# V rows of the paged cache loaded in single bundles among the K loads, and the mixer's steps in another order, in a one-core hybrid decoder step

## The reference, cut to what matters

```python
z = rmsnorm(x) @ w_in                  # 1024 x 3584: rq, rk, rv, rg (4 heads of 128), mq, mk, mv (8 heads of 64)
ret  = retention(rotary(rq), rotary(rk), rv)     # prompt: two chunks of 128; sample: 4 steps on state_ret
moba = block-sparse softmax attention(mq, mk, mv)
       # prompt: 256 own keys; sample: 2048 past keys from cache_k/cache_v by page_table:
       # the 3 best of 8 blocks of 256 (by q . mean k) and the own 4 keys
h = x + concat(norm(ret) * silu(rg), moba) @ w_out
y = h + moe(rmsnorm(h))                # top 4 of 32 experts, 1024 -> 2048 -> 1024
```

## Time and profile before

| | |
|---|---|
| median of 3 runs | 1317.4 us (1314.9 to 1321.56) |
| profiled execution, its own time | 1313.23 us |
| its span | 1311.3 us |
| busy: PE, DVE, ACT, POOL | 1222.4, 387.0, 232.3, 117.6 us |
| DMA moved | 500.64 MB, mean 382 GB/s |
| mixer and router, until the first expert's matmuls | 382.7 us |

### The profile page before, as it was taken

The page is one execution under the profiler, slowest core; times in us unless marked ns, Lnnn a source line. Parts: engine busy times, 40 slices in busy tenths (PEclk is TensorE's granted clock), DMA queues, the critical chain, the costliest instruction groups (busy, mean ns, idle before and its releaser), DMA issues.

```text
span 1311.3 us, 17401 instructions
## 1 busy us (share of the span) xinstructions
PE 1222.4 (93%) x7250; PEld 515.3 (39%) x7250; DVE 387.0 (30%) x551; ACT 232.3 (18%) x528; POOL 117.6 (9%) x117
## 2 busy tenths in 40 slices
PE   7999887658999999999999999999999999999996
PEld 3455443323553443434434343343434343343431
DVE  5999962205232211111211112211111112111113
ACT  3021141201421111101112011111201011211102
POOL 2222335263100000000000000000000000000000
PEclk8999998778999999999999999999999999999999
DMA  9999857873889999999999999999999999999994
GB/s 344 387 345 369 319 168 243 304 257 136 328 329 414 430 428 427 429 428 429 428 428 429 428 428 429 428 429 427 429 429 428 430 427 430 428 428 429 426 428 191
DMA packets 56316, 500.64 MB, mean 382 GB/s; under 512 B 6329, under 2 KB 6609, under 8 KB 27601
## 3 DMA queue, kind: packets, MB, share of 16 engines
q1 hardware_dynamic: 41840, 430.55, 78.4%
q0 software_dynamic: 14432, 69.47, 14.5%
...
## 4 chain that ended last, share of the span: by engine, by line
PE 59%; DMA 25%; DVE 9%; issue 5%; ACT 2%; POOL 1%; another core or an unknown queue 0%; SPq 0%; DVEq 0%; POOLq 0%; ACTq 0%
PE psum L904 22%; DMA arena<-w_gate_up 21%; PE psum L935 12%; DVE arena L1379 6%; PE psum L854 4%; PE psum L836 3%; DMA arena<-w_down 3%; PE psum L574 2%; PE psum L488 2%; PE psum L866 2%; PE psum L682 2%; PE psum L414 1%; PE psum L873 1%; PE psum L842 1%; POOL arena L1845 1%
## 5 line engine op out<-in xcount | busy, mean ns | idle before, releaser
L904 PE MATMUL psum<-arena 128*64 128x512 f32 x1920 | 422.7, 594 | 15.1 <-DMA arena<-w_gate_up 15.1
L904 PEld LDWEIGHTS psum<-arena 128*64 128x64 f32 x1920 | 134.9, 137 | 299.3 <-issue 264.6
L1699 DVE TENSOR_SCALAR arena<-psum 128x512 f32<-128x512 f32 x32 | 22.1, 692 | 682.2 <-PE psum L904 642.9
L935 PE MATMUL psum<-arena 128*64 128x512 f32 x960 | 212.6, 595 | 0.0
L1052 ACT ACTIVATE arena<-psum 64x512 f32<-64x512 f32 (+3 forms) x185 | 94.0, 510 | 406.1 <-PE psum L935 170.7
L1379 DVE STREAM_TRANSPOSE arena<-arena 128x2048 f32<-128x2048 f32 x32 | 121.6, 3946 | 2.7 <-PE psum L474 2.4
L935 PEld LDWEIGHTS psum<-arena 128*64 128x64 f32 x960 | 66.4, 137 | 124.1 <-issue 122.3
L488 PE MATMUL psum<-arena 128*128 128x512 f32 x224 | 107.2, 617 | 0.5 <-issue 0.4
L1270 ACT ACTIVATE arena<-arena 128x512 f32<-128x512 f32 x30 | 18.9, 631 | 418.8 <-DVE arena L1699 418.8
L1052 ACT ACTIVATE arena<-psum,arena 128x128 f32<-128x128 f32 (+2 forms) x182 | 53.8, 398 | 179.2 <-PE psum L488 124.6
L836 PE MATMUL psum<-arena 128*128 128x128 f32 x512 | 77.2, 294 | 0.0
...
## 6 DMA issues: line engine op xcount, KB each, us to landing
arena<-w_gate_up SPq DMA_DIRECT2D x128, 2048.0 KB, 29.7
...
arena<-cache_v,arena POOLq DMA_INDIRECT x64
```

The costliest lines, as they stand in the source:

```text
L904: last = mm(psum[64 * g:64 * (g + 1), b, :], xt[:, 2 * kk + m, lhs], gate_slot[slot][:, m, c:c + 512], start=False, stop=kk == 3 and m == ...
L935: last = mm(psum[64 * g:64 * (g + 1), 2, :], at_sb[:, m, SLOTS * q:SLOTS * (q + 1)], down_slot[slot][:, m, 512 * g:512 * (g + 1)], start=q ...
```

## The change

- V is loaded in single bundles, with a semaphore for each of twelve homes: eight in the K and V storage and four at word 12288, where the prompt scores go later. POOL's order is written out: K units 0 to 18, six V bundles, K units 19 to 24, then four V bundles and two K units in turn, then the rest of V. From unit 16 on K uses three homes instead of four, and two of its former places hold V.
- K units are spread over all 14 prompt parts (`K_PARTS`), and one V set is used at the end of each of the last six parts (`V_PARTS`).
- The sample's matmuls of blocks 1 to 6 stand between the k steps of the second prompt part, in bank 7, with semaphores of their own.
- `choose(0)` and both rotations stand between K transposes on DVE.
- The prompt scores and softmax come after block 6, their transposes and products after the retention products; value sets 8 to 15 stand among them. The transposed probabilities are written over the scores, and `state_ret` is loaded only after the prompt's products (`prompt_o`), since it shares their place.
- The new states of the sample are made two heads at a time, from k rows and v rows laid out on 128 partitions, so `v_blk` is made once. `k_dec` is cut to the prompt's two tiles.
- ACT's order follows PE's. What is computed is the same.

The diff, cut to its core (of code that only moved, the place where it now stands):

```diff
         DN = 16384
         kt_sb = at(DN, 2, 4 * 512)
         x_sb = at(DN + 4096, TILES, D)
-        pt_prompt = at(DN, 24, P)
         s_prompt = at(12288, 24, P)
+        pt_prompt = s_prompt
         rq_t = at(DN, RH, TOK)
         rk_t = at(DN + 1152, RH, TOK)
-        z_rg = at(DN + 3072, TILES, 512)
-        turn_2 = at(DN + 4608, TILES, RH, 64)
-        z_rv = at(DN + 5376, TILES, 512)
-        q_dec = at(DN + 6912, 2, RH, P)
+        q_dec = at(DN + 3072, 2, RH, P)
+        z_rg = at(DN + 4096, TILES, 512)
+        z_rv = at(DN + 5632, TILES, 512)
+        turn_2 = at(DN + 7168, TILES, RH, 64)
...
-        v_raw = at(KV, 2, 4, 2 * 512)
-        k_raw = at(KV, 4, 4 * 512)
+        k_raw = [at(KV + 2048 * i, 4 * 512) for i in range(4)]
+        v_raw = [at(KV + 1024 * i, 2 * 512) for i in range(8)] + [at(12288 + 1024 * i, 2 * 512) for i in range(4)]
...
-        UNITS_IN = (3, 3, 3, 3, 3, 4, 3, 3, 4, 3, 0, 0, 0, 0)
-        assert sum(UNITS_IN) == K_UNITS
+        K_HOME = [u % 4 if u < 16 else (u - 16) % 3 for u in range(K_UNITS)]
+        V_HOME = [(8, 9, 10, 11, 6, 7)[w % 6] if w < 24 else (2, 3, 4, 5, 0, 1, 6, 7)[w % 8] for w in range(4 * V_SETS)]
+        K_PARTS = (3, 3, 3, 3, 3, 2, 2, 2, 2, 2, 2, 2, 2, 1)
+        V_PARTS = (0, 0, 0, 0, 0, 0, 0, 0, 1, 1, 1, 1, 1, 1)
+        assert sum(K_PARTS) == K_UNITS
...
-                bank = (4, 6)[u // 4 % 2]
+                bank = 4 + u // 4 % 2
...
+            def v_set(n):
+
+                g, v, x = n // 8, n // 2, n % 2
+                if x == 0:
+                    pe.wait_ge(*mark[f"pt{v}_read"])
+                for w in range(4 * n, 4 * n + 4):
+                    pe.wait_ge(v_in[V_HOME[w]], 16 * loads(V_HOME, w))
+                for r in range(2):
+                    j = 2 * x + r
+                    for s in range(4):
+                        last = mm(psum[NS * s:NS * (s + 1), 6 + g, :],
+                                  pt_sb[:, v % 2, j * P + s:(j + 1) * P:4],
+                                  v_raw[V_HOME[4 * n + s]][:, 512 * r:512 * (r + 1)], start=False,
+                                  stop=n % 8 == 7 and r == 1, skip_group_check=True)
+                last.then_inc(v_used, 1)
+
+            def prompt_part(b, tile, sample=False):
+
+                part = 2 * b + tile
+                k_first, k_count = sum(K_PARTS[0:part]), K_PARTS[part]
+                v_first, v_count = sum(V_PARTS[0:part]), V_PARTS[part]
                 pe.wait_ge(win_in[b % 3], 16 * (b // 3 + 1))
                 w = win[:, b % 3]
                 A.wait_empty(pe)
                 bank = A.bank()
+                if sample and b > 1:
+                    pe.wait_ge(sample_empty, b - 1)
                 for k in range(KC):
                     last = mm(psum[:, bank, :], h_t[:, k, tile * P:(tile + 1) * P],
                               w[:, k, :], start=k == 0, stop=k == KC - 1)
                     if k == KC - 1:
                         n = A.filled(last)
-                    for u in range(first + units * k // KC, first + units * (k + 1) // KC):
+                    if sample:
+                        for j in range(4):
+                            last = mm(psum[NS * j:NS * (j + 1), 7, 0:P], h_t[:, k, LP:TOK],
+                                      w[:, k, j * P:(j + 1) * P], start=k == 0, stop=k == KC - 1)
+                        if k == KC - 1:
+                            last.then_inc(sample_full, 1)
+                    for u in range(k_first + k_count * k // KC, k_first + k_count * (k + 1) // KC):
                         k_unit(u)
+                    for u in range(v_first + v_count * k // KC, v_first + v_count * (k + 1) // KC):
+                        v_set(u)
                 return n
...
+                pe.wait_ge(d_empty, n_own)
+                pe.wait_ge(mvs_ready, 1)
+                for s in range(4):
+                    mm(psum[NS * s:NS * (s + 1), 6 + g, :], pt_own[0:NS, g, s::4],
+                       mv_s[0:NS, :], start=True, stop=False, skip_group_check=True)
...
+            mark["block0"] = (a_full, A.n)
+            prompt_part(1, 0)
+            prompt_part(1, 1, sample=True)
+            mark["block1"] = (sample_full, 1)
+            mark["z1"] = [(sample_empty, 1)]
+            pe.wait_ge(a_empty, mq)
+            slot_transposes(0)
+            prompt_part(2, 0)
+            pe.wait_ge(sample_empty, 1)
+            mkt = slot_transposes(1)
+            prompt_part(2, 1, sample=True)
+            mark["block2"] = (sample_full, 2)
+            mark["z2"] = [(sample_empty, 2)]
+            pe.wait_ge(q_own_ready, 1)
+            pe.wait_ge(a_empty, mkt[2])
...
+            prompt_part(3, 0)
+            prompt_part(3, 1, sample=True)
+            mark["block3"] = (sample_full, 3)
+            mark["z3"] = [(sample_empty, 3)]
+            p_transposes(0)
+            own_values(0, own_transposes(0))
+            prompt_part(4, 0)
+            prompt_part(4, 1, sample=True)
+            mark["block4"] = (sample_full, 4)
+            mark["z4"] = [(sample_empty, 4)]
+            p_transposes(1)
             prompt_part(5, 0)
+            prompt_part(5, 1, sample=True)
+            mark["block5"] = (sample_full, 5)
+            mark["z5"] = [(sample_empty, 5)]
+            p_transposes(2)
+            prompt_part(6, 0)
+            prompt_part(6, 1, sample=True)
+            mark["block6"] = (sample_full, 6)
+            mark["z6"] = [(sample_empty, 6)]
+            p_transposes(3)
+            values(6, 8)
             for u in range(6):
                 V.wait_empty(pe)
...
+            pe.wait_ge(rot_done, 2)
...
+            p_transposes(4)
+            po = own_transposes(1)
+            own_values(1, po)
+            values(8, 9)
+            evacuated(rt)
+            sc = []
...
+            values(9, 10)
+            p_transposes(5)
+            pe.wait_ge(kdec_ready, 1)
+            pe.wait_ge(sample_empty, 5)
...
+            values(10, 11)
+            pe.wait_ge(d_empty, sc[2])
+            pe.wait_ge(a_empty, n_st1)
+            retention_output(0)
+            retention_output(1)
+            o_transposes(0)
...
+            n_turned = ((A, A.n), (V, V.n))
+            p_transposes(6)
+            values(11, 12)
+            evacuated(n_turned)
+            pe.wait_ge(sample_empty, 2)
...
+            values(12, 13)
...
+            def sample_state(half, pair):
+                pe.wait_ge(vblk_ready, 1)
+                V.wait_empty(pe)
+                first, first_n = V.bank(), V.n + 1
+                V.n += 1
+                V.wait_empty(pe)
+                for h, bank in ((2 * pair, first), (2 * pair + 1, V.bank())):
+                    rows = slice(NS * h, NS * (h + 1))
+                    mm(psum[:, bank, :], k_rows_s[rows, :], v_blk[rows, 4 * half:4 * half + 4, :],
+                       start=True, stop=True).then_inc(d_full, 1)
+                V.n += 1
+                mark[f"state{half}{pair}"] = (d_full, V.n)
...
 
 
             attention, retention = range(4, 8), range(4)
             pe.wait_ge(s_evac, 8)
             evacuated(prompt_mix)
             pe.wait_ge(win_in[1], 16 * 3)
-            sample_state(0)
-            pt = p_transposes(6)
-            values(6, pt)
-            sample_state(1)
             output_part(0, 0, 4, attention)
-            pe.wait_ge(a_empty, n_st1)
-            retention_output(0)
-            retention_output(1)
-            pe.wait_ge(own_ready, 1)
+            p_transposes(7)
+            values(13, 14)
+            pe.wait_ge(state_in, 16)
+            sample_retention_output()
+            sample_state(0, 0)
             output_part(1, 0, 5, attention)
-            sample_state(2)
+            sample_state(0, 1)
+            values(14, 15)
             pe.wait_ge(o_norm, 1)
             pe.wait_ge(win_in[2], 16 * 3)
+            sample_state(1, 0)
             output_part(0, 1, 6, attention)
-            sample_state(3)
-            pt = p_transposes(7)
-            values(7, pt)
+            sample_state(1, 1)
+            values(15, 16)
...
+            k_transposes(18, 21)
+            own_reciprocal(0)
+            k_transposes(21, 23)
+            evacuate_own(0)
+            k_transposes(23, 25)
             rotate(rot_q, mark["z3"])
+            k_transposes(25, 28)
+            rotate(rot_k, mark["z4"])
+            k_transposes(28, K_UNITS)
+            choose(1)
+            qd = const("q_dec").rearrange("p (t h) -> p t h", t=TILES)
+            kd = const("k_dec").rearrange("p (t h) -> p t h", t=TILES)
+            dve.wait_ge(k_scored, K_UNITS)
+            v.tensor_tensor(q_dec, rot_q[:, 1:3], qd[:, 1:3].unsqueeze(3).broadcast_to([P, 2, RH, P]),
+                            ALU.mult).then_inc(qdec_ready, 1)
+            normalise(0)
+            dve.wait_ge(v_used, 6)
...
+            evacuate_own(1)
+            for h in range(RH):
```

(39 more changed lines are left out.)

415 lines of the change are left out of this document (149 added, 266 removed).

## The result

The changed kernel took 1325.8 us (median of 20 runs, 1319.75 to 1330.43) beside 1317.76 us for the kernel before in as many runs on the same chip. The ratio is 1.0053, 95% interval 1.0039 to 1.0067: 8.0 us slower, clear of noise though small, where 11.4 less had been forecast (1306.0; range 1286 to 1325). The profiled execution took 1323.63 us with a span of 1321.8, 10.4 and 10.5 more than the profiled execution of before.

The account below looks back on a forecast made before the run. The mixer's time before the first expert was taken to set the end, ahead of an untouched weight stream. 215.2 + 106 + 50.3 = 371.5 us against 382.7, 11.2 less, gave 1306 us; range 1286 to 1325.

Parts of the forecast that it names:

- the tail: From the last value set to the first expert: output projection and router, 50.3 us, left as it is by the change.
- POOL's queue: K units behind four V bundles in each of four rounds: 2 to 6 us to spare, so costed at nothing.
- Until block 6 ends: Mixer up to block 6's end: 20.0 us taken out, 21.5 added, so 215.2 us against 213.7 before.
- Samples between steps: Sample matmuls between k steps: six blocks with eight insertions at 0.20 us, 9.6 us added; ends 0 and 19.
- The second rival: Gain given back behind block 6, 1317 us, chance 0.16; insertions at double 0.20 would end block 6 9.6 us later, same time.
- `choose(0)`, 3.2 forecast: On DVE before K transpose 18: PE waits 3.2 us for K unit 18.
- `evacuate_own(0)`, 2.9 forecast: On DVE behind K transposes 21 and 22, with 22 waiting for unit 20's scoring: 2.9 us added.
- the third rival: K units behind four V bundles land in 10 us, not 5; four rounds add up to 20 us: 1326, chance 0.16.
- From block 6 to the last set: Stretch from block 6's end to the last value set: 106 us against 118.7 before.
- the state's 10.7: PE idle 10.7 us for `state_ret`, issued behind the prompt's products at 57 us after block 6, landing in 18.7.
- the sample retention 6: Sample retention behind block 6: 6 us taken, where it took 9.5 before and nine groups need 2.2.
- The end moves one for one with the first expert: Second part is an untouched weight stream, so the end follows the first expert's start, at 382.7 us before.

Follow-up runs that it names:

- e5: Changed kernel with the sample matmuls of blocks 1 to 6 in one run behind the k loop; ratio 1.0046 to the kernel before.
- e8: Changed kernel with the sample matmuls of two k steps together behind every second step, halving the insertions; ratio 1.0014 to the kernel before.
- e9: Changed kernel with each round's K units issued ahead of its V bundles on POOL's queue; ratio 1.0007 to the kernel before.
- f3: Changed kernel with samples behind the k loop, y's and the state's loads early, K units ahead of V bundles; 1290.1 us, ratio 0.9941 to the kernel before.
- c_after: The changed kernel itself, unedited, as a control on a chip where the kernel before takes 1300.1 us; ratio 1.0141 to the kernel before.
- f1: The changed kernel itself, unedited, as a control in a later group of runs; ratio 1.0128 to the kernel before.
- e1: Changed kernel with the sample state landing in the first w_in slot, its load issued when block 6 ends; ratio 1.0115 to the kernel before.
- e2: Changed kernel with y's memset and load put ahead of POOL's wait for the new states and their store; ratio 1.0054 to the kernel before.
- e3: Changed kernel with the first six V bundles issued behind K units 19 and 20, not ahead of them; ratio 1.0121 to the kernel before.
- e7: Kernel before with y's memset and load ahead of the state store, where the kernel before takes 1317.1 us; ratio 0.9989 to the unedited kernel before.
- c_before: The kernel before itself, unedited, profiled on a chip where it takes 1300.1 us; ratio 0.9995.
- f4: Kernel before with y's memset and load ahead of the state store, where the kernel before takes 1300.1 us; ratio 0.9951 to the unedited kernel before.

## Why the prediction was wrong, by its own steps

The forecast was 371.5 us for the first expert; it came at 392.7, 21 us later. Of this, 10.3 lie ahead of block 6's end, 3.3 behind it and 7.6 in the tail. Two steps had the mechanism wrong: the tail, taken as unchanged, and POOL's queue, costed at nothing. A third loss, the stall at 92 us, had no term.

**"Until block 6 ends": 215.2 forecast, 225.5 measured.**
- "Samples between steps, 9.6 us", and 1.2 for the value sets' insertions, were right by luck. The price was too low: an insertion costs 0.30 us by the spacing and 0.33 by the parts of e5 and e8, not 0.20. The count was too high: 36 and not 54, since twelve sample groups and all six value sets stand at steps that carry a K unit. 36 at 0.30 to 0.33 are 10.8 to 12 us, and 10.8 had been forecast. The 0.20 was the remainder of one spacing less durations read in other stretches; a K unit lasts 0.87 to 0.90 us where a value set follows it (164.10 to 164.97), not 0.98, and with that its own change costs 0.3 too. The Trainium skill, TensorEngine Tiling (Array Packing), section "Key Properties", says that changing the tiling mode drains the engine. By that rule the trace agrees that a change costs: the k steps with samples shown above are 1.41 us apart and not 1.11. That a drain makes it no run here shows. The second rival, which stood beside the rule, had the right direction in the price, with 0.40, and the same count of 48.
- `choose(0)`, 3.2 forecast, is the wait of 2.85 at 120.05. `evacuate_own(0)`, 2.9 forecast, is the 3.18 at 138.37 (DVE's two copies end at 138.3). Right.
- The transposes behind block 2's first part lost 4.4 us at 92 us, by a ScalarE that came late for nothing that the profile shows, and the two steps behind them ran at half clock, 4.9 us and not 2.8. No term had these 6.5 us; the stall appears only where the kernel before takes 1317 us, and its cause stays open. The first part of block 4, forecast to end at about 146, ended with its value set at 152.0.
- "POOL's queue, costed at nothing" failed. Unit 27 landed about 10 us after its issue and not 5, as the third rival had put it, and DVE waited 8.4 us. The 5 came from V bundles, which are half the size of a K unit; the median of the 32 K units is 7.9 us. But the four rounds did not add up to 20: PE waited 2.35 and 1.18 us, with half clock behind the first, and the second part of block 5 took 20.3 us where that of block 4, with the same work, took 14.8. e9 and f3 confirm that the order of K and V on this queue makes it, for 3 to 6 us. Beside a DVE rotation a K issue took 1.74 us and not 1.00 in c_after, like the V load of the earlier trace rows, too little to make K late.

**"From block 6 to the last set": 106 forecast, 109.3 measured, 103 to 104 in c_after, f1, e1, e2, e3 and e8.** The waits were foreseen: the state's 10.7 (11.41 measured, landing 19.3 for 18.7), the sample retention 6 (4.2). The state's load left 63.6 us behind block 6's end, not 57 (59.4 in c_after). The gain from 118.7 was real on the result's kind of chip only, for e7 has 118.8 there again; where the kernel before takes 1300 us it needs 103.4 (c_before) and 106.6 (f4), and nothing is won. Part of the 118.7 were the gaps between the sample retention's products, 7 us, which I read as the cost of the operation (9.5) and should have held against its own price (2.2).

**The tail, "which the change leaves as it is", 50.3: measured 57.9.** This step failed outright. The diff does not touch the projection, but it moves the new states to the end, POOL's 2 MB state store behind them, y's memset behind the store and y's load behind that. I counted the waits that PE would meet and did not follow the queue of POOL past the last thing that the diff edits. The trace of the kernel before had it. SP and DVE there:

```profile
332.21 0.37 SPq L1961 DMA_DIRECT2D arena<-x_prompt  x1
...
344.13 0.69 DVE L1596 TENSOR_TENSOR arena<-psum,arena 128x512 f32<-128x512 f32 x1 [8.10 <-DMA arena<-x_sample]
```

y's load left at the last set's end, with DVE already waiting 8.1 us for it, so its margin was thin. e2 shows the step that was missing: with y's load back ahead of the store the tail is 50.2.

**The sum and the rivals.** The errors are 10 + 3 + 8. The measured 1325.8 is all but the third rival's 1326, and that is chance: its mechanism was there with a quarter of its price, and the stall at 92 us, the late state load and y did the rest. "The end moves one for one with the first expert" held in all eighteen profiles.
